# Slot tables of all sixteen experts by eight products per layer, in a two-layer transformer with a routed feed-forward part

## The reference, cut to what matters

```python
glog = x @ wg + bg                                   # 4 groups
gp, gi = top_k(softmax(glog), 1)
elog = (x @ we + be)[group gi]                       # 4 experts in the chosen group
ep, ei = top_k(softmax(elog), 2); ep = ep / sum(ep)  # two choices per token
combine = sum over choices of one_hot(gi * 4 + ei) * (gp * ep)
h = silu(x @ w_gate[e]) * (x @ w_up[e]) * combine[e]   # 16 experts, width 256
out = sum over e of h @ w_down[e]
```

## Time and profile before

| what | us |
|---|---|
| median of the runs | 1982.55 |
| span of the profiled execution | 1984.4 |
| router, first layer: first operation of VectorE to the end of its last | 394.65 to 405.41 |
| experts, first layer: first comparison to the last scatter's start | 407.08 to 596.42 |
| experts, second layer, the same | 1020.27 to 1209.85 |
| TensorE busy over the span | 1707.1 (86%) |
| VectorE busy | 1153.0 (58%) |
| ScalarE busy | 901.3 (45%) |

### The profile page before, as it was taken

One profiled execution on the slowest core, in us unless ns is written; L12 is line 12 of the kernel. 1 busy time (PEld: TensorE's weight loads), 2 busy tenths in 40 slices (PEclk: granted clock), 3 DMA queues, 4 the chain that ended last, 5 costly groups with the idle time before them and its releaser, 6 DMA issues. The chain is left out here.

```text
span 1984.4 us, 22134 instructions
## 1 busy us (share of the span) xinstructions
PE 1707.1 (86%) x8018; PEld 1330.5 (67%) x8018; DVE 1153.0 (58%) x1721; ACT 901.3 (45%) x1371; POOL 634.5 (32%) x337
## 2 busy tenths in 40 slices
PE   5999997849982999988949992699896689999998
PEld 4876743748871876752737872587686578888887
DVE  3936565559975745746858985487455424233242
ACT  3246576238875235756327883435443331111112
POOL 2336632112211434731201210153622124444442
PEclk9999998969995999989969996799898899999999
DMA  4201011069954211020257983320000223222221
GB/s 186 85 32 45 30 57 64 12 275 346 374 216 187 97 54 45 1 70 16 85 210 305 365 324 131 132 97 31 21 1 1 85 109 115 90 101 102 90 85 43
DMA packets 40480, 233.93 MB, mean 118 GB/s; under 512 B 9316, under 2 KB 9700, under 8 KB 20660
## 3 DMA queue, kind: packets, MB, share of 16 engines
q1 hardware_dynamic: 31012, 215.46, 28.6%
q0 software_dynamic: 9216, 16.80, 2.3%
q10 hardware_dynamic: 144, 0.26, 0.1%
HBM read 226.03 MB, written 23.23 MB: 126 GB/s over the span
## 5 line engine op out<-in xcount | busy, mean ns | idle before, releaser
L259 PE MATMUL bank<-XS,WS 128*128 128x512 f32 x864 | 207.4, 403 | 15.8 <-DVE WS L384 15.8
L2561 POOL TENSOR_TENSOR WS<-ring,WS 128x2048 fp32r<-128x2048 f32 x31 | 149.3, 4817 | 188.2 <-ACT WS L2543 188.2
L259 PEld LDWEIGHTS bank<-XS,WS 128*128 128x128 f32 x864 | 166.0, 192 | 56.9 <-DVE WS L384 16.4
L1382 PE MATMUL bank<-WS,XS 128*128 128x512 f32 x768 | 189.1, 403 | 1.1 <-DVE XS L1502 1.1
L2543 ACT CAST WS<-ring 128x2048 fp32r<-128x2048 f32 x31 | 59.3, 1913 | 271.4 <-PE bank L2578 143.8
L2578 PE MATMUL bank<-XS,WS 128*128 128x512 f32 x768 | 174.9, 389 | 2.7 <-DVEq L2616 2.7
L2596 PE MATMUL bank<-WS,US 128*128 128x512 f32 x768 | 174.7, 389 | 0.0
L1382 PEld LDWEIGHTS bank<-WS,XS 128*128 128x128 f32 x768 | 146.1, 194 | 32.2 <-DVE XS L1502 1.9
L2578 PEld LDWEIGHTS bank<-XS,WS 128*128 128x128 f32 x768 | 144.1, 188 | 32.7 <-POOLq L2557 2.9
L2596 PEld LDWEIGHTS bank<-WS,US 128*128 128x128 f32 x768 | 144.2, 188 | 29.9
L1846 PE MATMUL bank<-XS,WS 128*128 128x512 f32 x576 | 135.6, 396 | 3.6 <-POOLq L2035 2.6
(11 more groups left out here) (531 smaller groups left out, 3486.4 us busy)
## 6 DMA issues: line engine op xcount, KB each, us to landing
raw<-in_w_exp SPq DMA_DIRECT2D x16, 2048.0 KB, 14.8
DN<-in_w_exp SPq DMA_DIRECT2D x32, 1024.0 KB, 10.5
ring<-in_w_ff SPq DMA_DIRECT2D x32, 1024.0 KB, 4.8
raw<-in_w_in SPq DMA_DIRECT2D x20, 1024.0 KB, 4.8
GU<-in_w_exp SPq DMA_DIRECT2D x8, 2048.0 KB, 17.1
XT<-in_w_exp SPq DMA_DIRECT2D x8, 2048.0 KB, 17.5
ring<-in_w_in SPq DMA_DIRECT2D x12, 1024.0 KB, 5.1
raw<-in_w_out SPq DMA_DIRECT2D x8, 1024.0 KB, 4.8
```

What stands on the lines that cost most here:

```text
L259: last = pe.matmul(m.ps[g % 8][:, :], WS[:, i % 2, hw, at:at + P], XS[:, hx, k, :], start=(step == 0), stop=(step == 3 * KD - 1))
L1382: last = pe.matmul(m.ps[2 + e % 2][:, :], r.XS[:, e % 2, hx, 4 * half + k, :], r.WS[:, half, hw, k * S:(k + 1) * S], start=(half == 0 and ...
L2561: pool.tensor_tensor(f.WS[:, q % 2, 1, :], f.ring[:, q % 4, :], f.WS[:, q % 2, 0, :].bitcast(F32), ALU.subtract).then_inc(w_low, 1)
```

## The change

The one-hot rows are built per choice in place of per expert. A token has exactly one slot for its first choice and one for its second, so one comparison per block of tokens and choice gives all that is needed: HOT is 128 tokens by 128 slots, eight of them per layer. VAL is masked, so that it has a token's numbers only in the column pair of the expert that it chose; the product HOT x VAL with 32 columns then adds a token to the right expert's table alone. Eight products summed in one bank give all sixteen tables, and one conversion writes them.

In the router OC (one-hot of the choice, over 16 experts), the masked VAL, SUM (running counts with a row of zeros ahead) and SLOT (a token's slot per choice, by a sum over the experts) take the place of SEC, POS and the unmasked VAL. In the experts stage all comparisons, products and the conversion come ahead of the loop; the loop has none left. The gathers wait for the one conversion.

```diff
+            link(dve.memset(r.SUM[:, 0, :], 0.0))
...
-            link(dve.tensor_tensor(by_group(r.SEC[:, :, :]), every_group(r.h2[:, :, :]), hot_group, ALU.mult))
-            link(dve.tensor_copy(r.VAL[:, :, :, 0], m.TOK[:, 0, :].rearrange("p (t a) -> p t a", a=1).to_broadcast([P, NT, NE])))
-            link(dve.tensor_tensor(r.VAL[:, :, :, 1], m.TOK[:, 1, :].rearrange("p (t a) -> p t a", a=1).to_broadcast([P, NT, NE]), r.SEC[:, :, :], ALU.add))
+            for c, choice in enumerate((r.h1, r.h2)):
+                link(dve.tensor_tensor(by_group(r.OC[:, c, :, :]), every_group(choice[:, :, :]), hot_group, ALU.mult))
+                for n in range(2):
+                    place = m.TOK[:, n, :].rearrange("p (t a) -> p t a", a=1).to_broadcast([P, NT, NE])
+                    link(dve.scalar_tensor_tensor(out=r.VAL[:, c, :, :, n], in0=place, scalar=float(c * n), in1=r.OC[:, c, :, :], op0=ALU.add, op1=ALU.mult))
...
-            link(dve.tensor_copy(r.SEC[:, 0, :], m.ps[3][:, 0:NE]))
-            for t in range(1, NT):
-                link(dve.tensor_tensor(r.SEC[:, t, :], m.ps[3][:, t * NE:(t + 1) * NE], r.SEC[:, t - 1, :], ALU.add))
+            for t in range(NT):
+                link(dve.tensor_tensor(r.SUM[:, t + 1, :], m.ps[3][:, t * NE:(t + 1) * NE], r.SUM[:, t, :], ALU.add))
...
-            link(dve.scalar_tensor_tensor(out=r.POS[:, :, :], in0=r.OH[:, :, :], scalar=-float(CHOSEN), in1=rank, op0=ALU.mult, op1=ALU.add))
-            link(dve.tensor_tensor(r.POS[:, 1:NT, :], r.POS[:, 1:NT, :], r.SEC[:, 0:NT - 1, :], ALU.add))
+            link(dve.tensor_tensor(r.OH[:, :, :], rank, r.SUM[:, 0:NT, :], ALU.add))
+            for c in range(2):
+                link(dve.tensor_tensor(r.OC[:, c, :, :], r.OC[:, c, :, :], r.OH[:, :, :], ALU.mult))
+            link(dve.reduce_sum(r.SLOT[:, :], r.OC[:, :, :, :].rearrange("p c t e -> p (c t) e"), AX.X))
...
-                pool.wait_ge(indexed, e + 1)
+                if e == 0:
+                    pool.wait_ge(indexed, 1)
...
-            for e in range(3):
-                table_of(e)
+            for n in range(2 * NT):
+                pe.wait_ge(hot_row, n + 1)
+                last = pe.matmul(m.ps[7][:, 0:2 * NE], r.HOT[:, n, :], r.VAL[:, n // NT, n % NT, :, :].rearrange("p e c -> p (e c)"),
+                                 start=(n == 0), stop=(n == 2 * NT - 1))
+            last.then_inc(table_done, 1)
...
-                if e == 0:
-                    table_of(3)
-                if e + 4 < NE:
-                    table_of(e + 4)
...
-            hot_rows(0)
-            hot_rows(1)
-            index(0)
-            hot_rows(2)
-            index(1)
-            index(2)
+            for n in range(2 * NT):
+                dve.tensor_scalar(r.HOT[:, n, :], m.IOTA[:, :], r.SLOT[:, n:n + 1], None, ALU.is_equal).then_inc(hot_row, 1)
+            dve.wait_ge(table_done, 1)
+            dve.tensor_scalar(r.TB[:, :, :].rearrange("p e c -> p (e c)"), m.ps[7][:, 0:2 * NE], float(NOWHERE), None, ALU.add).then_inc(indexed, 1)
```

More of the change, by code:

```diff
@@ L41 @@
 NE, FE = 16, 256
-CHOSEN, NOWHERE = 10000, 4096
+NOWHERE = 4096
 NGR = 4
@@ L123, in _ @@
             link(pool.affine_select(out=m.TRI[:, :], in_=m.ones[:, :], compare_op=ALU.is_gt, fill=0.0, base=0, pattern=[[1, P]], channel_multiplier=-1))
-            link(pool.iota(m.IOTA[:, :], pattern=[[1, P]], base=-CHOSEN, channel_multiplier=0, allow_small_or_imprecise_dtypes=True))
+            link(pool.iota(m.IOTA[:, :], pattern=[[1, P]], base=0, channel_multiplier=0, allow_small_or_imprecise_dtypes=True))
             for c in range(2):
@@ L1273, in _ @@
             dve.wait_ge(total_done, 1)
[L1274 to L1277 removed]
+            for t in range(NT):
+                link(dve.tensor_tensor(r.SUM[:, t + 1, :], m.ps[3][:, t * NE:(t + 1) * NE], r.SUM[:, t, :], ALU.add))
+            link(dve.reduce_max(r.NP[:, 0:1], r.SUM[:, NT, :], AX.X))
             link(dve.tensor_scalar(r.NP[:, 1:2], r.NP[:, 0:1], 128.0, 1.0, ALU.is_gt, ALU.add))
@@ L1530, in _ @@
             for e in range(NE):
[L1531 to L1534, removed]
                 if e + 1 < NE:
@@ L1544, in _ @@
                     low(e + 1, 1)
[L1545 to L1548, removed]
                 if e + 2 < NE:
@@ L1555, in _ @@
                 part_low(e)
-            dve.wait_ge(hot_row, NE * NT)
-            dve.tensor_scalar(r.POS[:, :, :], r.POS[:, :, :], -float(P), None, ALU.add).then_inc(dve_step, 1)
+            dve.wait_ge(hot_row, 2 * NT)
+            dve.tensor_scalar(r.SLOT[:, :], r.SLOT[:, :], -float(P), None, ALU.add).then_inc(dve_step, 1)
             dve.wait_ge(dve_step, 1)
@@ L2800, in build @@
                         r.XE = sb(nc, c3, "XE", P, 2, D)
[L2801 to L2804, removed]
+                        r.OC = sb(nc, c3, "OC", P, 2, NT, NE)
+                        r.SUM = sb(nc, c3, "SUM", P, NT + 1, NE)
+                        r.SLOT = sb(nc, c3, "SLOT", P, 2 * NT)
+                        r.VAL = sbr(nc, c3, "VAL", P, 2, NT, NE, 2)
+                        r.HOT = sbr(nc, c3, "HOT", P, 2 * NT, P)
                         r.NP = sb(nc, c3, "NP", P, 3)
```

## The result

The changed kernel took 1968.39 us (median of four runs, 1967.88 to 1972.31) against 1982.22 us for the kernel before in the same comparison: a ratio of 0.9937, interval 0.9921 to 0.9952. A second comparison with more runs gave 1971.31 against 1980.23 us, 0.9952, interval 0.9940 to 0.9964. So it is about 0.5% faster, 9 to 14 us. Forecast were 1976.0 us, a gain of 6.5 us, and a range from 1969: the first median lies 0.6 us outside, the second inside. The span of the profiled execution went from 1984.4 to 1970.6 us.

The account below looks back on a forecast made before the run. TensorE bounds the expert stage first, DMA from about 470 to 572 us. Per layer -4.3 (hole) - 0.55 (slack) + 1.6 (router) = -3.25 us; two layers -6.5 us, 1982.55 to 1976.0 us; range 1969 to 1983.

Parts of the forecast that it names:

- land at the same distance: Saturated part of the expert stage: ten loads following the first would still land 10.3 us apart, keeping the hole's gain.
- Hole: TensorE's 4.95 us pause after expert 1's transposes, awaiting expert 3's index conversion; shortening it gains 4.3 us per layer.
- a case with the lower clock: After the shortened pause the clock still drops, transposes and gate-up products take as long as before: 2.9 us gained.
- the two cases given: Second layer, gate-up products after the pause: 2.9 us gained if the clock drops, 4.4 or a little more if not.
- Slack behind the hole: End of the layer: half of the 1.1 us between the last load's landing and ScalarE's read, 0.55 us gained.
- Tables behind: Tables in TensorE's stream where the load queue is never empty: removal gains nothing, waits for gathered rows replace them.
- Router: VectorE's chain in the router: more operations and a memset add 1.6 us per layer, bounds 1.2 to 2.0.
- First gather: Opening of the expert stage: more comparisons and products start it 0.9 us later (0.6 to 1.3), TensorE's first work too.
- VectorE's cover: Expert rounds: VectorE loses about 1 us per expert, costed at nothing because TensorE does not wait for it there.
- first rival: Expert rounds: loads follow TensorE, DMA could serve 9.39 us per expert; -6.3 us per layer, 1970 us, chance 0.15.
- third rival: Stage opening: expert 2's rows land later, leaving only router and opening cost, 2.5 us per layer; 1987.6 us, chance 0.10.

Follow-up runs that it names:

- the second execution: The changed kernel run once more, unchanged, in a comparison with more rounds against the kernel before: 1971.3 us, ratio 0.9952.
- the hole alone closed: Kernel before, with expert 3's index conversion put ahead of the second weight subtraction on VectorE, all sixteen tables kept: 1972.3 us, ratio 0.9949.
- the hole back: Changed kernel, with TensorE in round 0 waiting for the second weight subtraction before expert 2's transposes, no table back: 1982.8 us, ratio 1.0004.
- three buffers: Changed kernel with gathers ahead of scatters, VAL made on GpSimd and a third buffer for results: 1969.5 us, ratio 0.9938.
- small loads: Changed kernel with the down loads of experts 2 to 15 cut to 256 of 2048 columns: 1961.6 us, ratio 0.9903.

## Why the prediction came out as it did

The mechanism was right in its main part: a hole at the head of each layer, and behind it a stage that DMA paces, where removed tables mostly buy waits. The forecast gain was too small by a quarter to a half. The step that failed is the sentence that the ten loads behind the hole "land at the same distance": they landed 10.03 and 10.18 us apart, not 10.30.

- **Hole.** Forecast -4.3 us per layer, as a mean of a case with the lower clock (-2.9) and one without (-5.7). Down 0 came 5.2 and 2.6 us sooner, and in the second execution 5.0 and 4.1; with the router's 1.4 us added back, 4.0 to 6.6 us, 5.6 on average. Three of four layers kept the clock up. The term was mis-sized since I gave the two cases equal weight, and since the first gather's landing did not move by its full 0.9 us (below). For the second layer the two cases given, 2.9 and 4.4 us, have a mean of 3.65, so even the sum as stated was 0.65 too high there.
- **Slack behind the hole.** Forecast -0.55 us. From down 0 to the layer's end it took 143.2 and 143.6 us before, 139.5 to 141.9 (mean 140.4) after, so -3.0 us. This is the term that failed most. The 1.1 us of margin at the last load shrank to 0.4, about as forecast; the rest is the distance of the landings. With the tables in, the loads of experts 5 to 15 landed 10.30 and 10.34 us apart before and 10.13 and 10.32 with the hole alone closed. With the tables out and the order of gathers and scatters kept, all sixteen full-size layers traced lie between 10.00 and 10.18. That is 0.2 us on average, 2 us over ten experts, and it goes with the tables, although it was forecast not to. Which part of a table does it is open: five or six products put back (10.00 to 10.14) and the comparisons alone (10.06 and 10.15) did not bring the longer distance back; the conversions were never put back. How much of the 3.0 us is the tables' share is open too: with the hole alone closed the stretch was 141.7 us in both layers, with the hole back and the tables out 138.5 and 141.5, and the changed kernel's own four values differ by 2.4.
- **Tables behind.** "I expect nothing" held for what was tested: putting the products of six or five of them back left the layer's end where it was. The distance of the landings above speaks for 2 us per layer that this does not cover. A table was worth 0.47 us to an unhindered round (9.75 to 9.28), not 0.36, since the down products behind it also took 0.1 us more; most of it went into waits, which came from expert 9 on; before, they came at experts 13, 14 and 15 in the first layer and 11, 14 and 15 in the second.
- **Router.** +1.6 forecast, +1.53 measured (406.94 against 405.41).
- **First gather.** +0.9 forecast, +0.73 from the first comparison to the gather's start; but the first transposes came 422.31 - 408.62 = 13.69 us after the first comparison, before 13.61. The later request landed faster, 10.3 us for 10.9, so nearly nothing reached TensorE.
- **VectorE's cover.** Nothing forecast, nothing seen in a round; up to 1 us per layer is not excluded.

By the terms: -5.6 - 3.0 + 1.4 = -7.2 us per layer against -3.25, or -14 us, of which the two timed comparisons show 9 to 14.

The time of the first rival, 1970 us, came closest, and its cause was not the one: if the loads had followed TensorE, rounds would have stayed at 9.3 us to the end, products put back would have cost 2 us and more, and smaller loads would have gained nothing. The time alone would have chosen the wrong story. Of the third rival, that only the opening's cost is left, the kernel with the hole back shows the first half: there is no gain. It was not slower by the 5 us that the rival forecast (1982.8 against 1981.55 us), so something paid for the router.

The Trainium skill, HBM Reference, section Specifications (TRN2), says that a core that streams alone measures well above its share of some 358 GB/s, about 425. This case's trace agrees at the opening of the stage, where the first weight loads are in flight: 422 GB/s. It does not agree for the rounds, where the core moved 371 GB/s at a DMA share of 0.96, and 395 in the best of the eleven stretches of ten microseconds from 451 to 561 us. One line for each:

```profile
412.00:422.00 10.00, 0.00 (x0) 0.00 (x0) 2.63 (x2) 3.70 (x2) 2.23 (x2) 0.50 1.00 422
501.00:511.00 10.00, 9.58 (x47) 7.81 (x48) 9.02 (x9) 8.70 (x11) 2.24 (x2) 1.00 1.00 395
```

An estimate from 425 GB/s is 8.6 us per expert and would have left TensorE the bound; the runs with three buffers and with small loads say it was not. Why the rounds move less than the opening at a nearly equal DMA share is not shown; gathers and scatters run beside the loads there.

## What to carry to other kernels

Look for the pause at the head of a stage before counting the work inside it: what opens a stage late delays everything that a saturated queue carries afterwards, clock included, while most of the work removed in front of a saturated queue turns into waiting. The distance of the landings is itself a measurement and not a constant: it moved by 0.2 us with the tables here, and ten times that is as much as a whole term of the sum. A growing time from issue to landing at a constant rate of requests shows the saturation long before any engine waits. And when a measured time fits a rival, put the removed work back in halves: where it stood tells more than how much it was.

## What the hardware did that I had not expected

- The gather of about 0.26 MB took from 4 us (nothing else queued) to 18 us (two loads of weights queued), and putting it ahead of the scatter only passed the delay on to the scatter: the median from issue to landing went from 14.4 to 12.2 us for the gathers of the first layer, and from 12.0 to 14.3 us for its scatters.
- GpSimd did four products of 128x64 in 1.04 us, 0.26 us each, where VectorE took 0.25 us. On 128x2048 the two are far apart in the trace of before: 4.82 us for GpSimd (L2561), 2.29 us for VectorE (L1496). Spans of GpSimd are rough in these traces.
- After pauses of 1.46, 1.80 and 1.88 us behind the transposes the granted clock stayed at 2.4 GHz in three layers of the changed kernel, and after one of 1.96 us it fell to 1.2 GHz; with the hole alone closed it fell after 2.01 us and stayed after 2.02. The fall in the changed kernel moved 24 products from 5.7 to 6.9 us and the first down products by 1.6 us. Between equal kernels this alone makes a difference of a microsecond or two in a run.
